# A long convolution by Fourier matrices: two stages made one, with even and odd tokens transformed apart

## What is computed

```python
def hyena_filters(n, P):
    ...
    filt = (hid @ P['hy_pos_w3']).reshape(n, HY_ORDER, 2, HY_WIDTH)
    filt = filt * jnp.exp(-t_norm[:, None, None, None] * jnp.abs(P['hy_decay']))
    fwd, bwd = filt[:, :, 0], filt[:, :, 1]
    taps = jnp.concatenate([fwd, jnp.zeros_like(fwd[:1]), jnp.flip(bwd[1:], axis=0)], axis=0)
    taps = taps / (jnp.sum(jnp.abs(taps), axis=0, keepdims=True) + EPS)
    return jnp.fft.rfft(taps, axis=0)

def hyena_mix(u, P):
    filt = hyena_filters(n, P)
    x1, x2, z = jnp.split(short_conv(u, P['hy_conv_w'], P['hy_conv_b']), 3, axis=-1)
    for o, gate in enumerate((x1, x2)):
        zf = jnp.fft.rfft(z, n=2 * n, axis=1)
        conv = jnp.fft.irfft(zf * filt[None, :, o], n=2 * n, axis=1)[:, :n]
        z = gate * (conv + skip[o] * z)
    return z
```

## Time and profile before

| | |
|---|---|
| three runs | 2685.82, 2695.11, 2701.06 us |
| median | 2695.11 us |
| the profiled execution's own time | 2691.1 us |
| its span, first to last instruction | 2689.2 us |
| mean granted TensorE clock | 0.912 of full speed |

### The profile page before, as it was taken

The page is one execution under the profiler, slowest core; times in us unless marked ns, Lnnn a source line. Parts: engine busy times, 40 slices in busy tenths (PEclk is TensorE's granted clock), DMA queues, the critical chain, the costliest instruction groups (busy, mean ns, idle before and its releaser), DMA issues. The chain is left out here.

```text
span 2689.2 us, 24221 instructions
## 1 busy us (share of the span) xinstructions
PE 2312.2 (86%) x9618; PEld 1693.8 (63%) x9618; DVE 1126.3 (42%) x1507; ACT 875.1 (33%) x1152; POOL 552.1 (21%) x174
## 2 busy tenths in 40 slices
PE   5889969978888899985999936889959998799997
PEld 2667744554333688764877734668728876588885
DVE  2444366623414312325888833550462223422223
ACT  3431113323111222223777722462433231322221
POOL 0320200031000244401000010343104441434340
PEclk8995989988989999986999968889979998899999
DMA  5222203310101323315999951222103231323210
GB/s 201 85 101 90 72 32 125 126 64 28 47 28 47 112 84 94 102 47 193 367 382 377 383 191 45 78 90 87 48 0 94 91 106 63 110 79 109 78 63 32
DMA packets 178832, 305.90 MB, mean 114 GB/s; under 512 B 9214, under 2 KB 67657, under 8 KB 178725
## 3 DMA queue, kind: packets, MB, share of 16 engines
q1 hardware_dynamic: 173028, 285.56, 31.1%
q0 software_dynamic: 3392, 10.48, 1.1%
q10 hardware_dynamic: 2304, 8.39, 0.8%
HBM read 281.27 MB, written 23.13 MB: 113 GB/s over the span
## 5 line engine op out<-in xcount | busy, mean ns | idle before, releaser
L130 POOL TENSOR_TENSOR region<-weights,region 128x2048 fp32r<-128x2048 f32 (+2 forms) x96 | 374.3, 3900 | 1166.0 <-ACT region L124 917.9
L236 PE MATMUL ps<-region 128*128 128x512 f32 (+1 forms) x1336 | 537.8, 403 | 80.9 <-PEq L2497 16.6
L239 PE MATMUL ps<-region 128*128 128x512 f32 (+1 forms) x1336 | 524.3, 392 | 0.0
L240 PE MATMUL ps<-region 128*128 128x512 f32 (+1 forms) x1336 | 523.9, 392 | 0.0
L236 PEld LDWEIGHTS ps<-region 128*128 128x128 f32 x1336 | 262.9, 197 | 146.4 <-issue 45.0
L239 PEld LDWEIGHTS ps<-region 128*128 128x128 f32 x1336 | 262.9, 197 | 54.7 <-issue 5.4
L240 PEld LDWEIGHTS ps<-region 128*128 128x128 f32 x1336 | 261.7, 196 | 51.5
L124 ACT ACTIVATE region<-weights 128x2048 fp32r<-128x2048 f32 (+2 forms) x98 | 158.4, 1621 | 327.2 <-PE ps L240 278.7
L2338 DVE TENSOR_TENSOR region<-weights,region 128x2048 fp32r<-128x2048 f32 x96 | 218.7, 2291 | 65.1 <-ACT region L2277 64.9
L277 PE MATMUL ps<-region 128*128 128x512 f32 x512 | 203.3, 397 | 24.5 <-POOL region L3107 21.9
L2277 ACT ACTIVATE region<-weights 128x2048 fp32r<-128x2048 f32 x96 | 183.8, 1917 | 82.9 <-DMA weights<-moe_w_up 29.2
(11 more groups left out here) (355 smaller groups left out, 2836.2 us busy)
## 6 DMA issues: line engine op xcount, KB each, us to landing
weights<-w_in SPq DMA_DIRECT2D x54, 1024.0 KB, 5.3
weights<-moe_w_gate SPq DMA_DIRECT2D x32, 1024.0 KB, 7.9
weights<-moe_w_up SPq DMA_DIRECT2D x32, 1024.0 KB, 8.9
weights<-moe_w_down SPq DMA_DIRECT2D x32, 1024.0 KB, 7.7
weights<-w_mod SPq DMA_DIRECT2D x24, 1024.0 KB, 5.2
weights<-w_mlp_in SPq DMA_DIRECT2D x16, 1024.0 KB, 5.2
weights<-w_mlp_out SPq DMA_DIRECT2D x16, 1024.0 KB, 5.0
h_slots<-region SPq DMA_DIRECT2D x16, 512.0 KB
```

The source lines that it names most:

```text
L130: eng.tensor_tensor(flat(self.part(K, n, 1)), flat(self.ring.view(n)), flat(self.part(K, n, 0)).bitcast(F32), ALU.subtract).then_inc(self. ...
L236: ins = pe.matmul(out, l_hi, r_hi, start=(start and k == 0), stop=False)
L239: pe.matmul(out, l_hi, r_lo, start=False, stop=False)
L240: ins = pe.matmul(out, l_lo, r_hi, start=False, stop=(stop and k == kt - 1))
```

## The change

One stage now does both orders. The tokens are kept in even and odd order (`phase_tokens`: tiles 0 and 1 hold even tokens, 2 and 3 odd ones). A transform is made at 256 frequencies of the even tokens (A: cosine, C: sine) and of the odd tokens (B, D) apart, two matmuls each, and the values at k and 512-k are sums and differences of these, made by VectorE (`add`). The product is formed on four blocks at a time, folded back to even and odd (`products`), and inverted at 256 frequencies (`inverse`; in order 1 with data as weights and 256 columns per matmul). The cosine and sine matrices are one chunk of the ring (`k_dft`), the inverse ones another (`k_idft`). Frequency 0 and the Nyquist and middle frequencies, which share row 0, are put right by six one-row products of GpSimd per order. The filter is no longer divided by its sum of magnitudes: the skip is multiplied by the sum instead (`patch`), and the last gate product multiplies by the reciprocal of both sums' product, as a column (`columns`, `scale`). The sums go to one row instead of 128. Filter weights, decays, skip and a table of order 0 are loaded by SP in `hyena_project_stage`, those of order 1 by SP at the stage's start, the decays already spread over the partitions. Filter pairs are handled as 1024-wide operations. The diff, cut to what the orders and costs need (the helpers for views, ScalarE's small functions and the host's tables are left out; ScalarE's own order has the same hand-written form):

```diff
+            for dst, src in ((w3, K.T["hy_pos_w3"][:, 0:1024]), (K.at(68, S)[0:1], K.T["hy_skip"][:, 0:S]),
+                             (dec.rearrange("p d c -> p (d c)"), K.T["hy_decay"][:, 0:1024].broadcast_to([P, 1024])),
+                             (K.hy_table[:, 0:264], K.T["k_hy_table"])):
+                sp.dma_start(dst, src).then_inc(filters_in, 16)
             r.issue_until(sp, n0 + 6 + RING)
+            sp.wait_ge(filters_in, 64)
...
-                    ins = pe.transpose(K.ps[:, 4 + q % 2, tt * P:(tt + 1) * P], y_of(t)[:, tt * P:(tt + 1) * P],
-                                       K.ident[:, :])
+                    ins = pe.transpose(K.ps[:, 4 + q % 2, tt * P:(tt + 1) * P], phase_tokens(y_of(t), tt), K.ident[:, :])
...
+def phase_tokens(v, t):
+    a = 256 * (t % 2) + t // 2
+    return v[:, a:a + 255:2]
...
+def hyena_stage(K):
+    QUADS = [("z", 0, 0), ("z", 0, 1), ("f", 0, 0), ("f", 0, 1), ("z", 1, 0), ("z", 1, 1), ("f", 1, 0), ("f", 1, 1)]
...
+            for o in range(2):
+                c0, d0, fc, fd = z_row[:, 0, :], z_row[:, 1, :], f_row[:, 0, :], f_row[:, 1, :]
+                n = 4 * o
+                pool.wait_ge(ev_d, reads_of_d[q_of("f", o, 0) + 1])
+                pool.wait_ge(rows, 2 * o + 2)
+                pool.tensor_tensor(a_row, c0, fc, ALU.mult).then_inc(chain, 1)
+                pool.wait_ge(chain, n + 1)
+                pool.tensor_tensor(fc, d0, fc, ALU.mult).then_inc(chain, 1)
+                pool.tensor_tensor(c0, c0, fd, ALU.mult).then_inc(chain, 1)
+                pool.wait_ge(chain, n + 3)
+                pool.tensor_tensor(fd, d0, fd, ALU.mult).then_inc(chain, 1)
+                pool.wait_ge(chain, n + 4)
+                pool.wait_ge(step, 14 * o + 7)
+                G = four(Z, 0)
+                pool.tensor_tensor(G[0:1, 1, :], a_row, fd, ALU.subtract).then_inc(fixed, 1)
+                pool.tensor_tensor(G[0:1, 3, :], c0, fc, ALU.add).then_inc(fixed, 1)
...
+            for dst, src in ((w3[1], T["hy_pos_w3"][:, 1024:2048]),
+                             (dec[1].rearrange("p d c -> p (d c)"), T["hy_decay"][:, 1024:2048].broadcast_to([P, 1024]))):
+                sp.dma_start(dst, src).then_inc(filters_in, 16)
+            sp.wait_ge(patched, 4)
+            sp.dma_start(skip, T["hy_skip"][:, S:2 * S]).then_inc(skip_in, 16)
+            r.issue_until(sp, n0 + 2 + RING)
...
+            def filters(o, i):
+                if o == 1 and i == 0:
+                    pe.wait_ge(filters_in, 32)
+                if o or i:
+                    pe.wait_ge(g_done, g_count(o, i - 1) if i else g_count(0, 3))
...
+                ins.then_inc(filt_done, 1)
+            def sums(o, i):
+                pe.wait_ge(abs_done, 4 * o + i + 1)
+                if o and i == 0:
+                    pe.wait_ge(scaled, 1)
+                for d in range(2):
+                    ins = pe.matmul(K.ps[0:1, B_SUM, :], K.ones[:, 0:1], pair_of(o, i)[:, d, :], start=(i == 0 and d == 0),
+                                    stop=(i == 3 and d == 1))
+                ins.then_inc(sum_done, 1)
...
+            def group(kind, o, j, part):
...
+                if q:
+                    if part == "D":
+                        pe.wait_ge(ev_d, reads_of_d[q])
+                    if part == "B":
+                        pe.wait_ge(ev_b, q)
+                    if part == "A":
+                        pe.wait_ge(added, 2 * q)
+                    if part == "C" and QUADS[q - 1][0] == "z" and QUADS[q - 1][2] == 0:
+                        pe.wait_ge(rows, 2 * o + 1)
...
+                pairs = []
+                for t in ((2, 3) if odd else (0, 1)):
+                    w = M[:, t, 256 * sine + j * P:256 * sine + (j + 1) * P]
+                    if kind == "f" and part == "C" and j == 0:
+                        w = c_zero[:, t, :]
+                    pairs.append((w, x[:, t, :]))
+                accumulate(pe, K.ps[:, bank, :], pairs).then_inc(tr, 1)
...
+            def inverse(o, j):
+                pe.wait_ge(step, 14 * o + 7 * (j + 1))
+                if j == 0:
+                    q = q_of("f", o, 1)
+                    pe.wait_ge(fixed, 2 * o + 2)
+                    pe.wait_ge(ev_d, reads_of_d[q + 1])
+                    pe.wait_ge(ev_b, q + 1)
+                    pe.wait_ge(added, 2 * q + 2)
+                G = four(Z, j)
+                for m in range(4):
+                    if o == 0:
+                        g = G[:, 2 * (m // 2):2 * (m // 2) + 2, :]
+                        for ri in range(2):
...
+                        for ph in range(2):
+                            for ri in range(2):
+                                ins = pe.matmul(K.ps[:, B_OUT[m], 256 * ph:256 * ph + 256],
...
+            filters(0, 0)
...
+            groups("z", 0, 0, "DB")
+            filters(0, 1)
+            groups("z", 0, 0, "AC")
+            filters(0, 2)
+            sums(0, 0)
+            groups("z", 0, 1, "DB")
+            filters(0, 3)
+            sums(0, 1)
+            groups("z", 0, 1, "AC")
+            sums(0, 2)
+            sums(0, 3)
+            groups("f", 0, 0, "DBAC")
+            edge(0)
+            columns(0)
+            filters(1, 0)
+            groups("f", 0, 1, "DBAC")
+            filters(1, 1)
...
+            inverse(0, 0)
+            sums(1, 0)
+            sums(1, 1)
+            inverse(0, 1)
+            filters(1, 2)
+            groups("z", 1, 0, "DB")
+            filters(1, 3)
+            groups("z", 1, 0, "AC")
+            sums(1, 2)
+            groups("z", 1, 1, "DB")
+            sums(1, 3)
+            groups("z", 1, 1, "AC")
+            groups("f", 1, 0, "DBAC")
+            edge(1)
+            columns(1)
+            groups("f", 1, 1, "DBAC")
+            inverse(1, 0)
+            inverse(1, 1)
...
+            def evict(kind, o, j):
+                q = q_of(kind, o, j)
+                act.wait_ge(tr, 4 * q + 1)
+                if j == 0:
+                    if kind == "z" and o:
+                        act.wait_ge(fixed, 2)
+                    act.activation((z_row if kind == "z" else f_row)[:, 1, :], K.ps[0:1, B_D, :], ACT.Copy).then_inc(ev_d, 1)
+                if q:
+                    act.wait_ge(added, 2 * q)
...
+                act.activation(ebd[:, 1, :], K.ps[:, B_D, :], ACT.Copy, **kw).then_inc(ev_d, 1)
+                act.wait_ge(tr, 4 * q + 2)
+                act.activation(ebd[:, 0, :], K.ps[:, B_B, :], ACT.Copy).then_inc(ev_b, 1)
...
+            def tap_pair(o, i):
+                g = pair_of(o, i)
+                dve.wait_ge(filt_done, 4 * o + i + 1)
+                dve.wait_ge(win_done, 4 * o + i + 1)
+                if i >= 2:
+                    dve.wait_ge(sum_done, 4 * o + i - 1)
...
+                    dve.tensor_tensor(g, K.ps[:, 0:2, :], win, ALU.mult).then_inc(g_done, 1)
+                if o and i == 0:
+                    dve.wait_ge(tr, 16)
+                dve.wait_ge(g_done, g_count(o, i))
+                dve.tensor_tensor(total[:, i, :], g[:, 0, :], g[:, 1, :], ALU.add).then_inc(td_done, 1)
+                dve.tensor_tensor(diff[:, i, :], g[:, 0, :], g[:, 1, :], ALU.subtract).then_inc(td_done, 1)
+            def patch(o):
+                n = 4 * o
+                dve.wait_ge(sum_done, 4 * o + 4)
...
+                dve.tensor_scalar(s_row, K.ps[0:1, B_SUM, :], EPS, None, ALU.add).then_inc(patched, 1)
+                dve.wait_ge(patched, n + 1)
+                dve.tensor_tensor(skip, skip, s_row, ALU.mult).then_inc(patched, 1)
+                dve.wait_ge(patched, n + 2)
+                dve.wait_ge(td_done, 8 * o + 8)
+                dve.tensor_tensor(total[0:1, 0, :], total[0:1, 0, :], skip, ALU.add).then_inc(patched, 1)
+                dve.tensor_tensor(diff[0:1, 0, :], diff[0:1, 0, :], skip, ALU.add).then_inc(patched, 1)
+            def add(kind, o, j):
+                q = q_of(kind, o, j)
+                d = four(Z if kind == "z" else F, j)
+                dve.wait_ge(ev_d, reads_of_d[q + 1])
+                dve.wait_ge(ev_b, q + 1)
+                dve.wait_ge(tr, 4 * q + 4)
...
+                dve.tensor_tensor(d[:, 0:2, :], K.ps[:, B_A:B_C + 1, :], ebd, ALU.add).then_inc(added, 1)
+                dve.tensor_tensor(d[:, 2:4, :], K.ps[:, B_A:B_C + 1, :], ebd, ALU.subtract).then_inc(added, 1)
+            def products(o, j):
+                z, f, n = four(Z, j), four(F, j), 14 * o + 7 * j
+                dve.wait_ge(added, 2 * q_of("f", o, j) + 2)
+                if n:
+                    dve.wait_ge(step, n)
+                dve.tensor_tensor(prod, z, f, ALU.mult).then_inc(step, 1)
+                dve.wait_ge(step, n + 1)
+                dve.tensor_tensor(z[:, 0::2, :], z[:, 0::2, :], f[:, 1::2, :], ALU.mult).then_inc(step, 1)
+                dve.tensor_tensor(z[:, 1::2, :], z[:, 1::2, :], f[:, 0::2, :], ALU.mult).then_inc(step, 1)
```

(95 more changed lines are left out.)

257 lines of the change are left out of this document (129 added, 128 removed).

## The result

The changed kernel takes 2586.97 us, the median of four runs (2575.12 to 2589.6); the kernel before took 2694.49 in four runs beside it (2685.82 to 2701.06). The ratio is 0.9596, with a 95% interval of 0.9579 to 0.9613. The profiled execution of the change took 2587.65 us.

What follows compares the result with a forecast made beforehand. TensorE was taken to bound the two stages, its own gaps doing the rest. 260.9 us minus a 152.2 us chain, less 0.3, saves 108: 2691.1 becomes 2583, plus 4.0 for the median gives 2587 us; range 2563 to 2612.

Steps and rivals of the forecast that it cites:

- The chain: New stage from first filter matmul to last scaled product, TensorE and VectorE legs: 140.4 us, 152.2 with locks and start clock.
- locks: VectorE and GpSimd operations with both inputs in SBUF wait for each other's whole instruction: 11.8 us added, 0 to 15.4.
- Work removed: TensorE work in the two replaced stages falls from 202 us to 113 us, 89 us less.
- u = 0.857: Time in us of one TensorE matmul of 512 columns at full clock, seen as two records of about 0.429.
- VectorE in the path: VectorE's 1024-element operations take 1.14 us back to back or 1.26 when awaited, a product quad 9.5; its sum is 90.
- Sums ahead of the first inverse: Order 1's sums wait for VectorE's magnitude ahead of the inverse on TensorE, until 67.0 us in the chain.
- The waits of order 1: TensorE waits twice in order 1 for VectorE's eviction, adds, taps and magnitude: 1.9 us each.
- The clock at the start: Half clock for up to 9 us at the stage's start costs 0 to 4.6 us; 1 was taken.
- Rival 2's smaller case: Half clock costs a third of 77 us where TensorE leads, giving 2612 us; rival 12%, most for this price.
- rival 3: GpSimd's twelve one-row operations and the locks become the path, making the kernel slower by over 13 us; 1%.
- rival 4: Work isn't removed as said, or chunks are delayed in the stage before: two thirds of the saving, 2623 us; 3%.
- the 0.3 for the strided transposes: Transposes reading every second token are at most 1.1 us dearer, most beside other work; 0.3 us was taken.

Runs made afterwards that it cites:

- experiment 3: Second half of order 0's inverse put ahead of order 1's sums, against the changed kernel: ruler 155.91 us, 2.2 less; kernel 2587.38 us.
- experiment 5: Three matmuls with unread results added between and after the projection stage's last transposes, against the changed kernel: ruler 156.21 us, 1.9 less; kernel 2583.54 us.

## Why the prediction was right, step by step

The saving predicted for the stages was 108.7 us and 107.0 were measured. The chain was 152.2 us from the first filter matmul; the last product ends at 154.6. Laid over the trace, in us:

| from, to | predicted | measured |
|---|---|---|
| first filter matmul, end of order 0's sums | 27.4 + 1 clock | 32.45 |
| product quad starts (684.83) | 11.8 | 11.74 |
| second sums of order 1 (717.29) | 34.2, 6.4 of it locks | 32.46 |
| quad of order 1 (761.58) | 43.1 | 44.29 |
| end of the quads (786.67) | 26.8, 5.4 of it locks | 25.09 |
| end of the last product (795.27) | 7.9 | 8.60 |

- **Work removed.** Record counts and u = 0.857 held; the second inverse runs at half a record each.
- **VectorE in the path.** 1024 columns at 1.22 (1.14 to the next start) against 1.26 and 1.14, a quad 9.4 against 9.5. The magnitude was 1.05 for 1.1.
- **Sums ahead of the first inverse.** TensorE did stand 2.04 us for them, though the first inverse half ran before the wait; experiment 3 takes it away. The waits of order 1 were 1.62 and 1.63, for 1.9 each.
- **Locks.** 11.8 predicted, 8.8 measured. All four of GpSimd's products were paid for in each quad, as the sum had it, but at less than the 1.28 us that it took for each: 0.79, 0.95, 1.06 and 1.06 in order 0. The first began 0.3 us ahead of the quad, and had 0.93 left to run. The mechanism was right and its size too large by 3.
- **The clock at the start.** The term "I take 1, since the gap before the stage shrinks to some 1.5 us" was mis-sized: 3.1. I looked at the gap alone. The stretch of transposes before it kept TensorE busy only half the time, and the clock had gone to 0.50 by the stage's first matmul, behind a gap of 1.11 us. The support for the term was also misread: the stretch from 657 to 680 of the earlier trace rows has no gap of 2 us. Its idle 2.3 us are three gaps of 0.76, of which this is one (the kernel before, timeline):

```profile
662.78 1.12 PE L1689 MATMUL ps<-region,ones 128*128 128x512 f32 x2 [0.76 <-ACT region L1744]
```

- **Switches between kinds of matmul.** Not in the sum at all. They made 1.9 us of the first line (29.3 in experiment 5, where the clock is full, against 27.4), and about 1.7 of the fourth, where the shorter waits hid part of them.
- **The clock inside.** After idle spans of 5.80 and 9.12 us TensorE ran at 0.50 from 699.5 to 708 and from 777.4 to 783 (stretches of the changed kernel, columns as above):

```profile
699.50:704.30 4.80, 3.78 (x4) 1.17 (x5) 4.72 (x5) 2.18 (x2) 1.86 (x2) 0.50 0.00 0
704.30:708.00 3.70, 3.68 (x5) 1.63 (x6) 3.67 (x3) 0.00 (x0) 0.00 (x0) 0.50 0.00 0
...
777.40:783.00 5.60, 5.57 (x13) 4.52 (x14) 5.57 (x4) 0.00 (x0) 0.00 (x0) 0.50 0.60 182
```

The Trainium skill (TensorE: Matmul & The Clock Gate, HAM oscillation — how this bites in real kernels) has waits between bursts put the clock back; by that rule, the trace agrees. But both spells lie beside VectorE's quads, the first at no cost, the second at some 0.6 us. Rival 2's smaller case, 2612, needed the low clock where TensorE leads, and there the third stretch read 1.00.

- **GpSimd as the bound** (rival 3) did not come near: with no GpSimd work at all the stage is 9.3 us shorter. **Work not removed** (rival 4) falls with the record counts and the time per record. The stage of the new loads kept its length, 76.70 us against 76.76, from its first matmul (563.47, before 559.50) to its last copy's end; the 0.3 for the strided transposes did not show.

Two misses of about 2 us each too low (clock, switches in order 0), 1.2 in order 1 and 0.7 at the end stand against 3 too high for the locks and small change: net 2.4. That they nearly cancel is luck, and that the median hits 2587 to the tenth is luck beyond that. The profiled execution took 2587.65 where the sum gave 2583. The projection stage began 4.0 us later, 3.0 of it in place by 77 us, where no instruction was changed.

In the nine traces with the new stage the projection stage begins between 560.66 and 563.75, in the two with the old one at 559.28 and 559.50. It is therefore not all scatter of one run. The traces show where the first 77 us grow by 1.0 to 3.4 us: a wait for the matrix `w_mod` ended after 4.49 or 4.50 us in all nine, and after 4.05 and 4.04 in the two, and in five of the nine, the change's among them, 16 small matmuls took 3.6 us instead of 1.95 (PE timelines, the kernel before and the change):

```profile
32.99 1.95 PE L319 MATMUL ps<-both,region 128*128 128x2 f32 x16
```

```profile
33.74 3.58 PE L319 MATMUL ps<-both,region 128*128 128x2 f32 x16
```

The granted clock beside them read 1.00 in both. Why wait and matmuls differ was not tried and stays open.

## What to carry to other kernels

When a stage becomes two engines taking turns, list which small helper work of a third engine starts together with the second one's leg, and move what feeds the helper earlier: here the two edge matmuls of each order, issued two groups sooner, were worth 6 us. Write the chain with a term for each switch of kind on TensorE (0.1 to 0.2 us), and look at what TensorE did before a stage, not only at the gap, to say at which clock it begins. Read an edit of a few us on a ruler inside the trace; single kernel times here moved by as much for other reasons.

## What the runs showed of the hardware

- GpSimd's product on one partition of 512 took 1.25 us, as much as its shortest 128-partition group.
- VectorE and GpSimd alternate on the lock one instruction each, so a short GpSimd operation can stretch from 1.25 to 3.19 us behind a 2048-wide VectorE one; VectorE paid 0.2 to 1.08 for a product of GpSimd, by how much of it was left.
- The granted clock at a stage's start followed the stretch ahead: 1.96 us busy of 3.8 left it at 0.50 for 6.4 us after a gap of 1.1 us, 3.48 of 3.8, with matmuls among the transposes, left it at 1.00 after a gap of 0.33. Gap and stretch changed together, so neither is shown to be the cause alone.
- A row of eight transform records costs 3.64 us to the next kind of matmul, one of sixteen 7.07: this switch has a fixed price of 0.21.
